# Two experts' rows kept on chip and spread by 0/1 products, the other fourteen gathered by index during the last expert, in a two-layer hybrid diffusion step

## The reference

```
t = h.reshape(B * S, D)
scores = jax.nn.sigmoid(t.astype(F32) @ router_w.astype(F32))
...
_, e_idx = lax.top_k(jnp.where(in_grp, sel, -jnp.inf), TOP_K)
w_sel = jnp.take_along_axis(scores, e_idx, axis=-1)
w_sel = w_sel / jnp.sum(w_sel, axis=-1, keepdims=True)
...
act = jax.nn.silu(g_) * u_ * gates[..., None].astype(t.dtype)
return jnp.einsum('tef,efd->td', act, w_down).reshape(B, S, D)
...
x = x + g2 * _moe(h2, router_w, router_b, lp['w_gate_up'], lp['w_down'])
```

## Time and profile before

| | |
|---|---|
| median of 3 runs | 1608.22 us (1606.21 to 1608.7) |
| profiled execution, its time | 1611.31 us |
| its span | 1608.4 us |
| PE busy | 1492.9 us (93%) |
| DVE busy | 1106.0 us (69%) |
| ACT busy | 914.9 us (57%) |
| mean granted PE clock | 0.962 |

### The profile page before, as it was taken

How to read it: one execution, slowest core, us unless ns; L and a number is a source line. 1 busy time by engine, 2 the same in 40 slices (tenths; PEclk the granted TensorE clock), 3 DMA queues, 4 the chain that set the end, 5 groups by cost and what they waited for, 6 DMA issues and landing times.

```text
span 1608.4 us, 19653 instructions
## 1 busy us (share of the span) xinstructions
PE 1492.9 (93%) x7453; PEld 1208.2 (75%) x7453; DVE 1106.0 (69%) x1691; ACT 914.9 (57%) x1151; POOL 152.7 (9%) x214
## 2 busy tenths in 40 slices
PE   6999999989986999999789999998998599999996
PEld 4699866679865888888569987665987478888875
DVE  4447657665556999999453665766465589999973
ACT  1323579952234787877322255998222387877761
POOL 1100022200011010000130001221000210000001
PEclk9999999989997999999889999998999799999997
DMA  9656431125566999999455553122431699999953
GB/s 355 224 200 210 157 112 61 61 105 183 194 260 224 381 412 410 404 407 400 164 186 173 200 191 127 61 99 71 146 116 76 255 358 404 407 407 408 408 231 131
DMA packets 133875, 377.21 MB, mean 235 GB/s; under 512 B 9352, under 2 KB 12816, under 8 KB 133776
## 3 DMA queue, kind: packets, MB, share of 16 engines
q1 hardware_dynamic: 113600, 326.04, 53.9%
q0 software_dynamic: 11152, 27.80, 4.8%
q10 hardware_dynamic: 9024, 22.03, 3.5%
HBM read 351.19 MB, written 24.66 MB: 234 GB/s over the span
## 4 chain that ended last, share of the span: by engine, by line
PE 83%; DVE 5%; issue 3%; ACT 3%; DMA 3%; POOL 1%; SPq 0%; POOLq 0%; ACTq 0%; DVEq 0%
PE bank L505 24%; PE bank L803 21%; PE bank L809 11%; PE bank L494 10%; PE bank L515 2%; PE bank L700 2%; PE bank L775 2%; DMA ring<-in_w_ada 2%; PE bank L892 2%; PE bank L673 1%; PE bank L531 1%; PE bank L610 1%; PE bank L605 1%; PE bank L524 1%; DMA gr<-h_rows,ids 1%
## 5 line engine op out<-in xcount | busy, mean ns | idle before, releaser
L1785 DVE TENSOR_TENSOR spot_low<-spot,piece_high 128x2048 fp32r<-128x2048 f32 x192 | 434.4, 2289 | 35.7 <-ACT piece_high L1199 34.3
L1199 ACT ACTIVATE piece_high<-spot 128x2048 fp32r<-128x2048 f32 x192 | 367.0, 1918 | 47.1 <-PE bank L809 45.8
L803 PE MATMUL bank<-piece_high,ga_r 128*128 128x512 f32 x768 | 310.7, 404 | 5.7 <-ACT gb L1223 2.4
L803 PE MATMUL bank<-spot_low,ga_r 128*128 128x512 f32 x768 | 303.6, 395 | 0.0
L809 PE MATMUL bank<-piece_high,ga_r 128*128 128x512 f32 x768 | 212.2, 398 | 0.0
L494 PE MATMUL bank<-hT,ring 128*128 128x384 f32 x576 | 197.7, 498 | 9.6 <-POOL hT L1901 5.5
L505 PE MATMUL bank<-parts_r,ga_r 128*128 128x384 f32 x768 | 202.6, 345 | 0.0
L803 PEld LDWEIGHTS bank<-piece_high,ga_r 128*128 128x128 f32 x768 | 145.6, 190 | 40.1 <-ACT ga_r L1204 3.0
L809 PEld LDWEIGHTS bank<-piece_high,ga_r 128*128 128x128 f32 x768 | 145.4, 189 | 35.0
L494 PEld LDWEIGHTS bank<-hT,ring 128*128 128x128 f32 x576 | 108.7, 194 | 82.3 <-issue 10.4
L803 PEld LDWEIGHTS bank<-spot_low,ga_r 128*128 128x128 f32 x768 | 145.7, 190 | 31.0
(11 more groups left out here) (282 smaller groups left out, 2261.4 us busy)
## 6 DMA issues: line engine op xcount, KB each, us to landing
spot<-in_w_gate_up SPq DMA_DIRECT2D x128, 1024.0 KB, 8.0
spot<-in_w_down SPq DMA_DIRECT2D x64, 1024.0 KB, 7.8
ring<-in_w_ada SPq DMA_DIRECT2D x24, 2048.0 KB, 8.1
ring<-in_w_in SPq DMA_DIRECT2D x22, 2048.0 KB, 8.0
expert_rows<-gb ACTq DMA_DIRECT2D x32, 512.0 KB, 6.9
ring<-in_w_attn_proj SPq DMA_DIRECT2D x4, 2048.0 KB, 8.7
ring<-in_w_rnn_proj SPq DMA_DIRECT2D x4, 2048.0 KB, 7.8
ring<-in_w_out SPq DMA_DIRECT2D x4, 2048.0 KB, 7.9
```

The source lines that it names most:

```text
L803: pe.matmul(out[n], high[:, 2 * q + k, :], w[:, k, n * 512:(n + 1) * 512], start=(q == 0 and k == 0 and i == 0), stop=False)
L1199: ac.activation(highs[p % HIGHS], spots[u], ACT.Copy).then_inc(S("piece_high"), 1)
L1785: ve.tensor_tensor(spots_low[u], spots[u], highs[p % HIGHS].bitcast(F32), ALU.subtract)\
```

## The change

Experts 14 and 15 (`HELD = 2`) are no longer stored. ACT copies their results from the banks, times the gate of each row, to a high part (`hold_y`), and DVE forms the low part (`low_of`); expert 15's down products go to banks `G` and no longer to `SB`. A matrix `select[i]` (128 places x 384 tokens, 0 or 1) is made on DVE during expert 4 (`places_of_rows`), and PE multiplies both parts with it (`spread`), which puts each row at its token.

POOL gathers the other rows as soon as the stores of experts 0 to 13 have landed; rows that belong to a held expert get place 0 and gate 0. ACT scales pick 0 by its gate (`scale_rows`), DVE adds pick 1 times its gate, and PE turns the sum into the same banks (`rows_in`, 3 transposes for each group of 128 features). Each group has a bank of its own (`sum_banks`), DVE adds it to `xT` with two instructions (`add_group`), and ACT squares it.

After layer 1 PE turns `xT` back half by half, ACT squares rows from the bank with an accumulated sum, and DVE multiplies by reciprocal root and gain in one instruction; the gain comes as a row by a load inside the experts of layer 1, and its early load goes. The spare blocks are now nested (`one_more`), so that one jump passes all five; they spread their rows in the same way, and the zeros go. PE reads the number of spare blocks ahead of expert 15's down products.

```diff
+HELD = 2
+SENT = NE - HELD
...
-        yg = [[(grf, gaf)[pick][:, t * 1024:(t + 1) * 1024] for pick in range(2)] for t in range(TT)]
-        diag = qT[:, :, :].rearrange("p h t -> p (h t)")[:, 0:2 * TT * P].rearrange("p (i c) -> p i c", c=P)
-        zrow = gbf[:, 2048:3072]
+        hT_rows = hT[:, :, :].rearrange("p k t -> p (k t)")
+        qT_rows = qT[:, :, :].rearrange("p h t -> p (h t)")
+        tmp_rows = tmp[:, :, :].rearrange("p i n -> p (i n)")
+        yg = [[hT_rows[:, 2048:3072], gbf[:, 2048:3072]],
+              [qT_rows[:, 768:1792], qT_rows[:, 1792:2816]],
+              [tmp_rows[:, 0:1024], tmp_rows[:, 1024:2048]]]
+        select = [qT_r[:, i, :] for i in range(HELD)]
+        held_high = [gbf_r[:, i * 1024:(i + 1) * 1024] for i in range(HELD)]
+        held_low = [flat_r("gr")[:, i * 1024:(i + 1) * 1024] for i in range(HELD)]
...
-        out_banks = SB + G
+        sum_banks = [OB, TB[0], TB[1], G[2], SB[0], SB[1], G[0], G[1]]
+        row_banks = [sum_banks[0:3], sum_banks[3:6]]
...
-            sy.dma_start(crow[16:24, :], final_norm_g.rearrange("(k p) -> k p", p=P)).then_inc(S("const_loaded"), 16)
...
+                pe.wait_ge(S("gates_placed"), l + 1)
+                for i in range(6):
+                    mm = pe.matmul(OB[0:CAP, 0:EVEN], hot_f[:, i, :], gate_b[:, i, :], start=(i == 0), stop=(i == 5))
+                mm.then_inc(S("gates_turned"), 1)
...
-                    if n >= 1:
+                    if n >= 1 and e < NE - 1:
...
+                        split_piece(f"dn{e}", SB if e < NE - 1 else G, by_k(actT_high, 4), by_k(actT_low, 4), q, 2,
...
-                dn(NE - 1)
                 pe.wait_ge(S("blocks_known"), l + 1)
                 more = pe.value_load(nri[0:1, 0:1], min_val=0, max_val=MORE)
-                for b in range(MORE):
+                dn(NE - 1)
+                def rows_in(g):
+                    if g == 0:
+                        pe.wait_ge(S("actT_low"), (l + 1) * NE)
+                        pe.wait_ge(S("rows_combined"), (l + 1) * TT)
+                    if g == 4:
+                        pe.wait_ge(S("y_copied"), (l + 1) * NE - 1)
+                        pe.wait_ge(S("held_low"), (l + 1) * HELD - 1)
+                    if g == 6:
+                        pe.wait_ge(S("y_copied"), (l + 1) * NE)
+                        pe.wait_ge(S("held_low"), (l + 1) * HELD)
+                    for t in range(TT):
+                        pe.matmul(sum_banks[g][:, t * P:(t + 1) * P], yg[t][1][:, g * P:(g + 1) * P], ident,
+                                  is_transpose=True, start=(t == 0), stop=False, skip_group_check=True)
+                def spread(g, i, last):
+                    for part in (held_high[i], held_low[i]):
+                        mm = pe.matmul(sum_banks[g][:, 0:T], part[:, g * P:(g + 1) * P], select[i],
+                                       start=False, stop=(last and part is held_low[i]), skip_group_check=True)
+                    return mm
+                for g in range(6):
+                    rows_in(g)
+                pe.wait_ge(S("selected"), l + 1)
+                pe.wait_ge(S("y_copied"), (l + 1) * NE)
+                pe.wait_ge(S("held_low"), (l + 1) * HELD)
+                for g in range(KT):
+                    if g >= 6:
+                        rows_in(g)
+                    for i in range(HELD):
+                        mm = spread(g, i, i == HELD - 1)
+                    mm.then_inc(S("group_done"), 1)
...
-                def combined(t):
...
+                        mm = square_sum(hT, g, slice(0, T), sq_base + KT + g + 1)
...
+                    pe.wait_ge(S("group_added"), l * KT + max(g, g // 4 * 3 + 2) + 1)
                     for t in range(TT):
-                        combined(t)
...
+                        mm = pe.transpose(row_banks[g // 4][t][:, g % 4 * P:(g % 4 + 1) * P],
+                                          xT[:, g, t * P:(t + 1) * P], ident)
+                    if g % 4 == 3:
+                        mm.then_inc(S("rows_turned"), 1)
...
+                def hold_y(i):
+                    e = SENT + i
+                    ac.wait_ge(S("piece_used"), PIECE_AT[(l, f"dn{e}.1")] + 1)
+                    ac.wait_ge(S(f"y_stored{e % 2}"), 16 * (l + 1) * SENT // 2)
+                    ac.activation(held_high[i].rearrange("p (i n) -> p i n", i=2), (SB_pair, G_pair)[i], ACT.Copy,
+                                  scale=slot_gate[:, e:e + 1]).then_inc(S("y_copied"), 1)
+                def scale_rows(t):
+                    ac.wait_ge(S(f"back{t}"), 32 * (l + 1))
+                    ac.activation(yg[t][0], yg[t][0], ACT.Copy, scale=gates[:, 0, t:t + 1]).then_inc(S("rows_scaled"), 1)
...
-                copy_y(NE - 2)
                 copy_act(NE - 1)
-                store_y(NE - 2)
-                copy_y(NE - 1)
-                store_y(NE - 1)
-                for b in range(2):
-                    ac.wait_ge(S(f"y_stored{b}"), 16 * (l + 1) * NE // 2)
-                ac.nop().then_inc(S("experts_done"), 1)
+                hold_y(0)
+                for t in range(TT):
+                    scale_rows(t)
+                hold_y(1)
+                ac.activation(smx[:, 0, 7:8], ones[:, 0:1], ACT.Sqrt)
...
+                def row_squares(half, t):
+                    n = half * TT + t
+                    return ac.activation(hT_rows[:, n * 512:(n + 1) * 512], row_banks[half][t][:, :], ACT.Square,
+                                         accum_out=row_sums[half][:, t:t + 1])
+                ac.wait_ge(S("rows_turned"), 1)
+                for t in range(TT):
+                    ins = row_squares(0, t)
+                ins.then_inc(S("first_sums"), 1)
+                ac.wait_ge(S("rows_turned"), 2)
+                ac.wait_ge(S("first_half"), 1)
+                for t in range(TT):
+                    link(row_squares(1, t))
+                    ac.activation(row_sums[3][:, t:t + 1], row_sums[1][:, t:t + 1], ACT.Sqrt,
+                                  bias=row_sums[2][:, t:t + 1], scale=1.0 / D).then_inc(S("final_rms"), 1)
...
-            ve.memset(zrow, 0.0)
...
-                def gate_diagonals():
-                    for i in range(2 * TT):
-                        pick, t = divmod(i, TT)
-                        ins = ve.tensor_scalar(diag[:, i, :], ident, gates[:, pick, t:t + 1], None, ALU.mult)
-                    ins.then_inc(S("diag_ready"), 1)
...
+                def places_of_rows():
+                    keep, place_f = p2(2), p2(3)
+                    link(ve.tensor_scalar(keep, blk, float(SENT), None, ALU.is_lt))
+                    ve.tensor_tensor(gates[:, :, :], gates[:, :, :], keep, ALU.mult)
+                    link(ve.scalar_tensor_tensor(place_f, blk, float(CAP), row, ALU.mult, ALU.add))
+                    link(ve.scalar_tensor_tensor(posu[:, :, :], place_f, 1.0, keep, ALU.mult, ALU.mult))
+                    ve.nop().then_inc(S("places_known"), 1)
+                    for i in range(HELD):
+                        link(tokens_of(i, SENT + i))
+                        ins = choose(i)
+                    ins.then_inc(S("selected"), 1)
...
+                def low_of(i, pair, gate):
+                    high = held_high[i].rearrange("p (i n) -> p i n", i=2)
+                    return ve.scalar_tensor_tensor(held_low[i].rearrange("p (i n) -> p i n", i=2), pair, gate,
+                                                   high.bitcast(F32), ALU.mult, ALU.subtract)
+                for t in range(TT):
+                    ve.wait_ge(S("rows_scaled"), l * TT + t + 1)
+                    ve.scalar_tensor_tensor(yg[t][1], yg[t][1], gates[:, 1, t:t + 1], yg[t][0], ALU.mult, ALU.add)\
+                        .then_inc(S("rows_combined"), 1)
+                for i in range(HELD):
+                    ve.wait_ge(S("y_copied"), l * NE + SENT + i + 1)
+                    low_of(i, (SB_pair, G_pair)[i], slot_gate[:, SENT + i:SENT + i + 1]).then_inc(S("held_low"), 1)
+                def add_group(g):
+                    for st in range(2):
+                        ins = ve.scalar_tensor_tensor(xT[:, g, STREAM[st]], sum_banks[g][:, STREAM[st]],
+                                                      modA[:, 3, g, st:st + 1], xT[:, g, STREAM[st]], ALU.mult, ALU.add)
+                    return ins
+                for g in range(KT):
+                    ve.wait_ge(S("group_done"), l * KT + g + 1)
+                    add_group(g).then_inc(S("group_added"), 1)
...
+                ve.wait_ge(S("first_sums"), 1)
+                ve.tensor_scalar(row_sums[2], row_sums[0], 1.0 / D, EPS, ALU.mult, ALU.add).then_inc(S("first_half"), 1)
+                ve.wait_ge(S("gain_loaded"), 16)
+                for t in range(TT):
                     ve.wait_ge(S("final_rms"), t + 1)
-                    ve.reciprocal(rms_c[:, 1, t:t + 1], rms_c[:, 0, t:t + 1]).then_inc(S("final_rstd"), 1)
...
+                    link(ve.reciprocal(row_sums[4][:, t:t + 1], row_sums[3][:, t:t + 1]))
```

(16 more changed lines are left out.)

251 lines of the change are left out of this document (107 added, 144 removed).

## The result

The changed kernel takes 1585.8 us at the median (1581.0 to 1587.4, 4 runs) against 1608.2 before (1606.2 to 1608.7): a ratio of 0.986 [0.984, 0.988]. The forecast was 1575.8 and 1570.5 to 1583, so the sign is right and the time lies 10 us above the forecast, 2.8 above the top of its range. The profiled execution is the slowest of the four: it took 1587.4 with a span of 1585.5; before, 1611.3 and 1608.4. So the span fell by 22.9 us where the working has 32.4, and 9.5 us are to be found.

What follows compares the result with a forecast made beforehand. It took the late gathers and the chain behind each layer's last expert as the bound. Gains of 17.1 (layer 0), 15.0 (layer 1) and 0.3 (start) sum to 32.4 us: 1575.8 from 1608.22, range 1570.5 to 1583.

Steps and rivals of the forecast that it cites:

- The early gathers: Behind the last expert, POOL's six gathers start at 1553.4 in place of 1574.50; the last is issued at 1559.6.
- M': Mark at the last expert's end: forecast as ACT's last copy starting, 0.47 us sooner; measured as the last down product's end.
- the copy order: Before the last down products, ACT copies the turned activations first, so PE starts 0.47 us sooner.
- the end: Layer 1's output after the last expert: span ends at M' + 24.35, a gain of 14.95 us.
- The table load of 1.28 in layer 1: ACT's load ahead of the output's root costs 1.28 us, root directly behind; the skill's 1.38 us drain is left out.
- the tail: Layer 1's small serial output steps, squares, roots and DVE passes, ending at M' + 24.35; called the least certain term.
- the jump: PE's jump over spare blocks, before layer 0's sums and layer 1's transposes: 0.2 us; even 3.13 hidden by the sequencer's lead.
- the count of the sums: PE's sums of squares at layer 0's end: eight at 0.34 us, 2.7 us, root at M' + 12.1.
- rival 1: Sequencer held by waits in the spreading, so the jump shows: 2.9 us more per layer, 1581.6; chance 18%.
- the limit: Last gather may land until about 1566.7, M' + 2.6 - 5.0, without delaying the spreading; slack 1.4 us.
- rival 2: Gathers end last, through a slower store and landing: 2.8 us more per layer, 1581.4; chance 12%.
- The two rivals together: Both the jump showing and the gathers ending last: 1587; chance 2%.

Runs made afterwards that it cites:

- the run with the three edits: Changed kernel with PE's branch turned round, DVE's last low pieces in quarters, and expert 14's low part and PE's transposes reordered tile by tile: 1573.4 us, 0.980.
- the second profile: The changed kernel run again with no edit, for another profile: 1581.8 us, ratio 0.985 to the kernel before.
- the run in one pass: On top of the run with the three edits, layer 0's squares and the ones as rounded fp32, one pass per sum: 1569.3 us, 0.977.

## Why the prediction was wrong

**What held.** The early gathers as the source of the gain (the run that delays them loses it all); their start, 15.4 us before M' (15.7 forecast); the copy order, PE 1.28 us behind the turning's start and not 1.81 (0.47 forecast, 0.53 measured); spreading 6.5 us long (6.4); PE's clock, 1.00 where it was 0.50; the end at M' + 24.8 (24.35), with luck (below). The table load of 1.28 in layer 1 stands 0.01 us behind the accumulator's read and 0.02 ahead of the root: no drain of 1.38 on top, so there the row was right, and the figure of the Trainium skill (ScalarE: Activation LUTs, What ACT_TABLE_LOAD costs), cited in the working, was not seen.

The end is right by two errors that cancel. Spreading was 1.8 late and the jump showed 0.6. Against that the tail was reckoned about 2.1 too long, as the run with the three edits shows: its spreading starts at 2.6 as forecast, and it ends at M' + 22.2. Three squares took 1.8 in place of 2.85, and each tile on DVE 1.5 in place of 1.83.

Three steps failed. In layer 0, where the error is, they are worth 3.4 us (the jump, and 1.7 more by the clock that fell behind it), 2.7 (the count of the sums) and 1.7 (the gathers). Experiments took them away in turn: without the jump the root came at M' + 16.2 in place of 21.5, with the gathers on time too at 14.3, with half the records too at 11.8.

**"So a jump of 3.13 begins at M' + 5.9 and is over when the products are."** This step cost most. The mechanism was right: the sequencer leads by some 3 us and hides that much. It began 2.9 us before the spreading ended (799.6 against 802.5). But the jump takes 6.28 us in layer 0, twice the longest row of before, since its target's fetch starts 3.7 us late beside the next layer's weights. 3.4 showed in layer 0 and 0.6 in layer 1; rival 1 had 2.9 in each, for another reason (a sequencer held by the waits in the spreading, which the early start of the jump rules out). In this execution the clock then fell, 1.7 more; in another with the same hole it did not.

**"8 x 0.34 (16 products took 5.43) = 2.7".** The row has x16 for matmuls in fp32, and a sum of 384 columns in fp32 is two of them. The eight sums are sixteen records, 5.4 us; 2.7 us of the shortfall is a misread count. The run with the three edits shows it: with no hole and no late spreading its root is at M' + 14.3, 2.2 past the forecast. That the run in one pass has its root at M' + 11.8, close to the forecast's 12.1, is chance: its sums took 2.0 us and not 2.7, and the root waited for the table load.

**"Six took 6.22 us from first to last issue ... so the last goes at 1559.6".** That row is from a time when DVE was idle. The new place of the gathers is beside DVE's low pieces, where three of them waited for a running low piece, and they took 8.7 us. The landing moved from M' - 3.8 to M' - 0.6, past the limit (M' - 2.4) by 1.7 to 1.8 in each layer: rival 2's mechanism (gathers last), by another cause than its late store. The limit itself was right: the 5.0 us that it allows behind the landing are the 5.0 that the first profile shows. In the other phase of DVE's work, as in layer 0 of the second profile, the last gather is issued at M' - 8.9 and the limit is kept.

**Start.** The forecast had M' of layer 0 come 0.8 us sooner. It came at 791.6 in the first profile and at 786.8 to 791.6 in the twelve of the changed kernel and its variants (788.8 at the middle), against 791.4 and 790.0 in the two of before: some 2 us may have been won, but with this spread that is not shown. **Loop.** From the root to M' the first profile won 1.7 us, 1.2 more than the copy order explains; over all variants it took 746.5 to 749.2, before 749.4 and 749.7. Why was not tried.

The two rivals together had been given 2%, as if each needed its own accident. Their sum, 1587, was the closest of the figures, partly by luck: the misread count is not in it. What is left open: why the clock fell behind the same 3.4 us hole in some executions and not in others, and what moves the start and the loop from one execution to the next.

## What to carry to other kernels

A row's duration is tied to what ran beside it: when a step is moved, look at what its new neighbours do to it, here POOL's issues beside DVE's passes with two SBUF inputs (0.94 to 2.9 us) and a jump beside weight loads (3.4 to 6.3 us). Put the rare case's code in the branch that is jumped to, so that the usual case runs straight on and the long jump lies where the engine waits anyway. Count records against instructions before a rate is used: here an fp32 product is two records, an fp32 transpose or an fp32r product one.

## What the runs showed of the hardware

- Most jumps on PE over one block took 0.21 to 0.37 us. Those with an instruction transfer inside were long: 2.8 to 3.2 in the kernel before (one block, one in each layer), 3.3 to 3.8 over five blocks, and 6.1 to 6.3 beside weights at 388 GB/s, where the transfer starts 3.5 to 3.7 us after the jump and not 0.9. In between were two, 1.8 and 1.4, in layer 0 of the kernel before; what made them is not shown.
- A gather's issue waits for DVE's running instruction with two SBUF inputs, and ends 0.8 to 0.9 us behind it (up to 2.9 us in all); beside a pass with one input from a bank it took 0.94.
- The same idle stretch of 3.4 us on PE was followed by a granted clock of 0.50 in some executions and of 1.00 in others, and the sums took 7.1 or 5.4 us.
- ACT's table load runs while PE sums, costs 1.28 us, and in layer 0 showed only when the sums were cut from 5.3 to 2.0 us.
